# Rotary queries and keys read from PSUM, gains in the tables, and half of a projection moved behind the first attention heads

## What is computed

```
proj = h @ w_in[l]                                   # 1024 -> 1536, split into qa ka va qb kb vb
qa = apply_axial_rope(rms_norm_2(qa, qn_g[l]), cos, sin)    # 8 heads of 64
ka = apply_axial_rope(rms_norm_2(ka, kn_g[l]), cos, sin)    # 2 heads of 64
oa = global_attention(qa, ka, va)                    # softmax of q.k / 8, no mask
ob = window_sink_attention(qb, kb, vb, sink[l], slopes)     # 8 heads, distance bias, a sink
mix = concat(rms(oa), rms(ob)) @ w_o[l]
h = layer_norm(ALPHA * h + mix);  h = layer_norm(ALPHA * h + peer_ffn(h, ...))
```

## Time and profile before

| | |
|---|---|
| median of 3 runs | 2634.62 us |
| the profiled execution: time | 2633.16 us |
| its span | 2631.3 us |
| PE busy | 2512.1 us (95%) |
| DVE busy | 1767.3 us (67%) |
| ACT busy | 1240.7 us (47%) |
| POOL busy | 504.8 us (19%) |
| mean granted TensorE clock | 0.972 |
| HBM | 159 GB/s over the span |

### The profile page before, as it was taken

How to read it: one execution, slowest core, us unless ns; L and a number is a source line. 1 busy time by engine, 2 the same in 40 slices (tenths; PEclk the granted TensorE clock), 3 DMA queues, 4 the chain that set the end, 5 groups by cost and what they waited for, 6 DMA issues and landing times.

```text
span 2631.3 us, 43837 instructions
## 1 busy us (share of the span) xinstructions
PE 2512.1 (95%) x17391; PEld 2262.1 (86%) x17391; DVE 1767.3 (67%) x3113; ACT 1240.7 (47%) x2661; POOL 504.8 (19%) x387
## 2 busy tenths in 40 slices
PE   7898999999899999999999999799999999999997
PEld 6768897998679999999888887679999999888886
DVE  4647334445668975888777556668975888777556
ACT  5441134445345454444555555345454444555554
POOL 3600143544436600000000000536600000000000
PEclk9999799999899999999999999899999999999999
DMA  5400034664324566556678665314566655688664
GB/s 176 134 3 1 25 104 153 185 191 156 109 59 151 163 183 181 184 184 183 208 237 244 198 195 172 112 49 152 163 183 182 184 183 181 207 244 242 197 193 150
DMA packets 146027, 421.09 MB, mean 160 GB/s; under 512 B 15904, under 2 KB 49056, under 8 KB 145440
## 3 DMA queue, kind: packets, MB, share of 16 engines
q1 hardware_dynamic: 142032, 405.34, 50.8%
q0 software_dynamic: 2192, 8.99, 1.0%
q10 hardware_dynamic: 1600, 3.96, 0.4%
HBM read 400.40 MB, written 17.83 MB: 159 GB/s over the span
## 4 chain that ended last, share of the span: by engine, by line
PE 76%; DVE 16%; DMA 3%; ACT 2%; issue 1%; POOL 1%; DVEq 0%; ACTq 0%; SPq 0%
PE pb L418 75%; DMA raw<-in_vT 2%; PE pb L427 2%; DVE arena L2039 1%; DVE arena L2031 1%; DVE arena L2033 1%; DVE arena L2062 1%; DVE arena L2036 1%; DVE arena L2028 1%; DVE arena L1430 1%; DVE arena L1860 1%; ACT hi L1015 1%; DVE arena L1433 1%; DVE lo L1440 1%; DVE arena L1580 1%
## 5 line engine op out<-in xcount | busy, mean ns | idle before, releaser
L1015 ACT CAST hi<-raw 128x512 fp32r<-128x512 f32 x1402 | 815.3, 620 | 409.1 <-DMA raw<-in_vT 187.0
L418 PE MATMUL pb<-HTh,hi 128*128 128x256 f32 (+1 forms) x2968 | 860.6, 290 | 9.9 <-DVE lo L1440 9.9
L418 PE MATMUL pb<-HTl,hi 128*128 128x256 f32 (+1 forms) x2968 | 844.9, 285 | 0.0
L418 PE MATMUL pb<-HTh,lo 128*128 128x256 f32 (+1 forms) x2968 | 844.4, 284 | 0.0
L1440 DVE TENSOR_TENSOR lo<-raw,hi 128x1024 fp32r<-128x1024 f32 x476 | 579.9, 1220 | 92.4 <-ACT hi L1015 92.4
L2201 POOL TENSOR_TENSOR lo<-raw,hi 128x512 fp32r<-128x512 f32 x359 | 487.9, 1382 | 576.7 <-ACT hi L1015 576.2
L418 PEld LDWEIGHTS pb<-HTh,hi 128*128 128x128 f32 x2968 | 573.1, 193 | 12.4 <-issue 10.4
L418 PEld LDWEIGHTS pb<-HTl,hi 128*128 128x128 f32 x2968 | 573.5, 193 | 0.9
L418 PEld LDWEIGHTS pb<-HTh,lo 128*128 128x128 f32 x2968 | 572.5, 193 | 0.0
L418 PE MATMUL pb<-hi,WH 128*128 128x512 f32 x1112 | 434.5, 391 | 7.4 <-DVE WL L2165 7.4
L418 PE MATMUL pb<-lo,WH 128*128 128x512 f32 x1112 | 433.5, 390 | 0.0
(11 more groups left out here) (191 smaller groups left out, 2310.2 us busy)
## 6 DMA issues: line engine op xcount, KB each, us to landing
raw<-in_uT SPq DMA_DIRECT2D x256, 512.0 KB, 3.7
raw<-in_vT SPq DMA_DIRECT2D x256, 512.0 KB, 4.3
raw<-in_w_ffn_in SPq DMA_DIRECT2D x44, 512.0 KB, 3.6
raw<-in_wq SPq DMA_DIRECT2D x32, 512.0 KB, 3.7
wk<-kept SPq DMA_DIRECT2D x128, 128.0 KB, 4.3
raw<-in_w_in SPq DMA_DIRECT2D x24, 512.0 KB, 4.0
raw<-in_w_ffn_out SPq DMA_DIRECT2D x22, 512.0 KB, 4.3
raw<-in_w_gate SPq DMA_DIRECT2D x16, 512.0 KB, 3.5
```

What stands on the lines that cost most here:

```text
L418: return e.matmul(o, l, r, start=start, stop=stop)
L1015: e.copy(u.hi[k], u.half[k]).then_inc(*s.up("hi", ("hi", g)))
```

## The change

- The queries' and keys' rotation reads the projection from PSUM. The gains are multiplied into cosine and sine tables (RC, RS), which POOL makes once a layer (`tables`). The sine part takes two instructions per half instead of four. ACT no longer copies queries and keys; it squares them from PSUM, and for the keys it also sums.
- The queries stay without their norm. Its inverse root goes into the exponential's scale (one value per token and head), and into the factor that makes the negated maximum. In the diff below the programs of PE (`tensor`), ACT (`scalar`), DVE (`vector`) and POOL (`gpsimd`) follow each other; left out are the root, reciprocal and two scalings of the queries, and the keys' mean, rotation, sum and norm, which stand in the same form. The keys are scaled by theirs after the rotation.
- The last two units of the third projection are multiplied in heads 0 and 1; its result goes to banks 4 and 5, and the first attention's output to 6 and 7. The last unit of the second projection comes after the query tiles. The warm matmuls ahead of the heads and in the first two go; tiles 9, 5 to 8 are turned in heads 5 to 9.
- The two broadcast DMAs come after POOL's splits for the projections; one more unit of w_o is cast and split ahead during the heads.
- POOL makes u's low parts up to unit 23; picks run from unit 24 to 48, the gates at 54.

```diff
-            add(("u", l, j), d["uT"][l, j], low=pool if j < 18 else dve)
+            add(("u", l, j), d["uT"][l, j], low=pool if j < 24 else dve)
...
+        self.qneg = self.s2.rearrange("p t h -> p h t")
+        self.RC, self.RS = (T["wk"][:, i * 256:i * 256 + 256].rearrange("p (w t e) -> p w t e", w=2, t=2) for i in range(2))
...
-        project(0, 4)
-        project(1, 6)
...
-        project(2, 0, q_tiles)
+        for g in range(4):
+            project(0, g, 4)
+        for g in range(3):
+            project(1, g, 6)
+        for f in range(4):
+            turn_tile(f, ("qa", l))
+        project(1, 3, 6)
+        for g in range(2):
+            project(2, g, 4)
         turn_tile(4, ("ka", l))
-        warm(5, 6)
...
-            if h < 5:
-                turn_tile((9, 5, 6, 7, 8)[h], ("qb", l))
+            if h < 2:
+                project(2, 2 + h, 4)
+            if 5 <= h < 10:
+                turn_tile((9, 5, 6, 7, 8)[h - 5], ("qb", l))
             if 1 <= h <= 16:
                 at_turn(h - 1)
-                warm((h - 1) % 2, 5)
+                if h > 2:
+                    warm((h - 1) % 2, 5)
...
-            e.copy(m.PJ[:, t, 0:512], PB[4 + t][:, :]).then_inc(*s.up("qkv2", ("pj", l, 0, t)))
+            w.wait_ge(*s.to("q_rope", l, t))
+            fn(m.PJ[:, t, 0:512], PB[4 + t][:, :], ACT.Square).then_inc(*s.up("qkv2", ("pj", l, 0, t)))
...
+            for k in range(2):
+                x = fn(m.PJ[:, t, 512 + 64 * k:576 + 64 * k], PB[6 + t][:, 64 * k:64 * k + 64], ACT.Square, acc=m.ss[:, t, 8 + k:9 + k])
+                x.then_inc(*s.up("qkv2", *([("k_sq", l, t)] if k else [])))
+        w.wait_ge(*s.to("k_ms", l))
+        fn(m.rs[:, :, 8:10], m.s2[:, :, 8:10], ACT.Sqrt).then_inc(*s.up("roots", ("k_root", l)))
+        for t in range(2):
+            w.wait_ge(*s.to("k_rope", l, t))
+            e.copy(m.PJ[:, t, 640:768], PB[6 + t][:, 128:256]).then_inc(*s.up("qkv2", *([("va", l)] if t else [])))
...
-                x = fn(m.PX[i][:, t * 256:(t + 1) * 256], sv[:, t, :], ACT.Exp, bias=m.nmx[:, h, t:t + 1], scale=0.125,
-                       acc=m.den[:, h, t:t + 1])
+                x = fn(m.PX[i][:, t * 256:(t + 1) * 256], sv[:, t, :], ACT.Exp, bias=m.nmx[:, h, t:t + 1],
+                       scale=0.125 if g else m.rs[:, t, h:h + 1], acc=m.den[:, h, t:t + 1])
...
+            if h == 2:
+                second_group()
+            elif h == 9:
+                split_high(units.i + 3)
...
+        def rotate(t, h0, h1, src, which, *done):
+            n = h1 - h0
+            cs = slice(64 * h0, 64 * h1)
+            sx = m.RS[:, which, t, :].rearrange("p (a s i) -> p a s i", a=2, s=2)
+            q5 = src.rearrange("p (h a s i) -> p h a s i", h=n, a=2, s=2)
+            r5 = QR[:, t, cs].rearrange("p (h a s i) -> p h a s i", h=n, a=2, s=2)
+            w.wait_ge(*s.to("tables", l))
+            own()
+            for si in range(2):
+                x = tt(r5[:, :, :, si, :], q5[:, :, :, 1 - si, :], sx[:, :, si, :].unsqueeze(1).to_broadcast([128, n, 2, 16]), M)
+                x.then_inc(*up("rope"))
+            co = m.RC[:, which, t, :].unsqueeze(1).to_broadcast([128, n, 64])
+            tt(heads(QK[:, t, cs], n), heads(src, n), co, M).then_inc(*up("rope", *done))
...
+        for t in range(2):
+            w.wait_ge(*s.to("pj_ps", l, 0, t))
+            rotate(t, 0, 8, PB[4 + t][:, :], 0, ("q_rope", l, t))
+        q_sum()
+        for t in range(2):
+            w.wait_ge(*s.to("pj", l, 0, t))
+            e.tensor_reduce(m.ss[:, t, 0:8], heads(PJ[:, t, 0:512], 8), AXX, A).then_inc(*up("rope"))
+        mean(0, 8, "q_ms")
...
+    tables(0)
     spread(0, m.bc, d["ln_in_g_2"], d["ln_in_b_2"])
     for l in range(2):
-        w.wait_ge(*s.to("turn", ("in", l), 7))
-        spread(2 * l + 1, m.bc1, d["ln1_g_2"][l], d["ln1_b_2"][l])
         for i in range(3):
             for g in range(4):
                 take("win", l, i, g)
+        w.wait_ge(*s.to("turn", ("in", l), 7))
+        spread(2 * l + 1, m.bc1, d["ln1_g_2"][l], d["ln1_b_2"][l])
+        split_low(units.i + 3)
```

More of the change, by code:

```diff
@@ L827, in tensor, with project @@
         turned(("in", l), m.Hv, lambda t, k: ("hn", 2 * l, t, k), range(8), 4, low=False)
[L829 to L846, removed]
+        def project(i, g, b0):
+            u = units.take("win", l, i, g)
+            for k in range(2):
+                c = 2 * g + k
+                for t in range(2):
+                    emptied(b0 + t)
+                    w.wait_ge(*s.to("lo", u.g[k]))
+                    w.wait_ge(*s.to("turn", ("in", l), c))
+                    x = mm3(PB[b0 + t][:, :], m.pair(m.HT, ALL, c, slice(t * 128, (t + 1) * 128)), u.part(k), c == 0, c == 7)
+                    if t == 1:
+                        x.then_inc(*s.up("part", ("part", u.g[k]), *([("pj_ps", l, i, t)] if c == 7 else [])))
+                    elif c == 7:
+                        x.then_inc(*s.up("part", ("pj_ps", l, i, t)))
+                    if c == 7:
+                        free[b0 + t] = [("pj", l, i, t)]
         def turn_tile(f, ready):
@@ L968, in tensor @@
             u_step(j)
-            if j == 50:
+            if j == 54:
                 for p in range(3):
@@ L1298, in scalar, with second_group @@
         take("win", l, 2, 1)
[L1299 to L1308, removed]
+        def second_group():
+            for t in range(2):
+                w.wait_ge(*s.to("pj_ps", l, 2, t))
+                src = PB[4 + t][:, 0:256].rearrange("p (j e) -> p j e", j=4)
+                e.copy(qb[t][:, 1, :, :], src).then_inc(*s.up("qkv2"))
+                e.copy(m.QP[:, t, 1152:1280], PB[4 + t][:, 256:384]).then_inc(*s.up("qkv2", *([("qb", l)] if t else [])))
+                e.copy(m.PJ[:, t, 1408:1536], PB[4 + t][:, 384:512]).then_inc(*s.up("qkv2", ("pj", l, 2, t), *([("vb", l)] if t else [])))
         def at_scores(h):
@@ L1823, in heads @@
             return a.rearrange("p (h e) -> p h e", h=n)
[L1825 to L1831, removed]
         def mean(h0, h1, step):
@@ L2209, in spread, with tables @@
         e.dma_start(bc[:, 1024:2048], b.partition_broadcast(128)).then_inc(*s.up(f"bc{n}", ("bc", n), by=16))
+    def tables(l):
+        co = m.C("cos").rearrange("p (t e) -> p t e", t=2)
+        si = m.C("sin").rearrange("p (t a s i) -> p t a s i", t=2, a=2, s=2)
+        for k in range(2):
+            gain = m.bcs[:, 136 * l + 64 * k:136 * l + 64 * k + 64]
+            ga = gain.rearrange("p (a s i) -> p a s i", a=2, s=2)
+            rs = m.RS[:, k, :, :].rearrange("p t (a s i) -> p t a s i", a=2, s=2)
+            tt(m.RC[:, k, :, :], co, gain.unsqueeze(1).to_broadcast([128, 2, 64]), M).then_inc(*s.up("tables"))
+            for h in range(2):
+                x = tt(rs[:, :, :, h, :], si[:, :, :, h, :], ga[:, :, 1 - h, :].unsqueeze(1).to_broadcast([128, 2, 2, 16]), M)
+                x.then_inc(*s.up("tables", *([("tables", l)] if k and h else [])))
     d = m.d
```

108 lines of the change are left out of this document (45 added, 63 removed).

## The result

The changed kernel takes 2611.05 us (median, 2608.6 to 2613.05), the kernel before in the same runs 2633.36: a ratio of 0.991, 95% interval 0.9888 to 0.9932. It is faster by 22 us, where 59 were forecast (2634.6 - 2576), and lies outside the range. The profiled execution has a span of 2609.9 us, 21.4 less than before.

The account below looks back on a forecast made before the run. PE was taken to bound the kernel, busy 95% of the span. Gains of 21.1 and 21.7 (attention, two layers), 2.6 (output projection) and 13.6 us (experts) sum to 59.0: 2576 us against 2634.6, range 2568 to 2598.

Parts of the forecast that it names:

- POOL's earlier start and the rotation from PSUM: Before the heads: POOL begins 1.3 us earlier, first projection ends T0 (last state split's end) + 7.3; DVE's rotation takes 3.0.
- The query sums: Attention's front, DVE: four sums in POOL's pause take 1.43 us and end 11.9 us after T0.
- rival A: Attention's front: query sums and key products still stall beside POOL's splits, giving 2590 to 2594 us; chance 0.12.
- The queries' scales: Attention's front, DVE: the queries' root, reciprocal and two small scalings end 14.7 us after T0.
- The fourth scores: PE, fourth head: scores end at T0 + 38.3, against 60.1 before in layer 0 and 60.7 in layer 1.
- The softmax scale: Heads, ACT: the exponential's per-partition scale costs 0, covered by ACT's 2.23 us idle before a head's first exponential.
- The expert stage: Experts: six more units split by POOL remove PE's 4.9 us wait and lost clock; 13.6 us gained over two layers.
- Three more tiles ... now lie behind this point, 0.22 each: Heads: five tiles instead of two are turned after the fourth head's scores, costing 0.22 us each.
- The 0.66: Chance given to the forecast of 2576 us, with its own range 2568 to 2585.
- Rival B: Clock: PE's short stops before the heads and missing warm matmuls cost 5 us a layer, giving 2586; chance 0.08.
- no pause of 9 us, so the heads run at 2.4 GHz: Heads: without the former long PE wait the clock stays up; about 6 us of each layer's front gain.
- the output projection, 2.6: Output projection: the third w_o unit, cast and split early, cuts PE's waits for POOL; 2.6 us gained over both layers.

Follow-up runs that it names:

- E4: Changed kernel with the expert stage put back: POOL splits u to unit 17, picks from unit 18, gates at 50; 2622.0 us, ratio 0.9957.
- E1: Changed kernel with only the PSUM bank of the five late tiles changed, to the one the previous head's transposes don't use; 2581.5 us, ratio 0.9804.
- E7: E3 without the third unit of w_o cast or split during the heads; 2579.1 us, ratio 0.9805.
- E5: Changed kernel, shared bank kept, with the warm matmuls put back in the first two heads and ahead of the heads; 2615.7 us, ratio 0.9935.
- E9: Changed kernel, shared bank kept, with nine matmuls on constants placed in the tile waits of heads 6 to 9; 2595.5 us, ratio 0.9861.
- E8: Kernel before the change, with the tiles of heads 1 to 4 moved to the bank the previous head's transposes use; 2653.0 us, ratio 1.0088.
- E2: Changed kernel with only the output projection's banks changed, from 0, 1, 4, 5 to 0, 1, 6, 7; 2606.8 us, ratio 0.9893.
- E12: E1 with only head 6's tile sharing its bank with the transposes of head 5; 2589.4 us, ratio 0.9826.
- E11: E7 with two warm matmuls a head instead of five; 2572.2 us, ratio 0.9767.
- E3: Changed kernel with both bank edits, late tiles (E1) and output projection (E2); 2580.3 us, ratio 0.9792.

## Why the prediction was wrong

**Right.** POOL's earlier start and the rotation from PSUM: T0 + 6.8 and 2.8 us against 7.3 and 3.0. The query sums at 12.6 against 11.9 (rival A's stretch, small: 3.00 instead of 1.43). The queries' scales came at T0 + 17.5 against 14.7; three instructions of 128x16 elements (L1445) beside POOL's splits took 3.1 us of that. The fourth scores at 39.6 and 41.2 against 38.3; of the 2.9 missing in layer 1, 1.7 is a half-clock stretch of 3.4 us at 1648.6. The softmax scale: the exponential grew from 0.47 to 0.56 us and ACT still idles 1.83 before it. The expert stage: 13.9 against 13.6, and E4 gives 14.1 in the traces.

**Wrong: "Three more tiles ... now lie behind this point, 0.22 each".** This is the step that failed. I priced the moved tiles by PE's time alone (0.22 is right: E1's heads with a tile take 3.25, those without 3.03) and did not list what they are queued against: the PSUM bank of each, by head, and the DVE instruction that frees it. The 0.66 was about 15: E1, which changes nothing but the bank, takes back 14.3 and 14.0 a layer, and with it the total, 2581.5, comes within 6 us of the forecast. The loss adds up: 17.1 and 18.6 us a layer are missing up to head 15's scores; 1.3 and 2.9 were missing at the fourth scores, 14.3 and 14.0 are the bank, 1.3 and 1.5 the early unit of w_o (E1 against E7). Rival B had the form (a stretch at half clock in the heads), but put it behind the pauses ahead of the heads and the missing warm matmuls, at 5 us a layer and a chance of 0.08. The pauses ahead of the heads cost 1.7 us of clock at most, the missing warm matmuls were not the cause (E5), and the price was three times as high: 9 us of clock and some 5 of waiting. The sentence "no pause of 9 us, so the heads run at 2.4 GHz" fails with it: two pauses of 0.94 stood before the fall, and PE was busy for 10.11 of the 12 us.

The traces show waits of 0.94 us in successive heads with 24 us at half clock behind them, and none at half clock up to head 15 when the waits are filled or cut to 0.87 (E9). The sentence of the Trainium skill that stands beside rival B ("TensorE: Matmul & The Clock Gate", section "A second HAM failure mode: psum-queue depth-cycling") says of frequent short idle times between groups of matmuls that the clock swings with them; the changed kernel agrees (23.9 us at 0.50 in each layer), E8's layer 1 doesn't (1.00 with four such stops). I weighed it by the rows of before, which had no such waits in the heads; the question was which new ones the moved work would make there.

**Wrong: the output projection, 2.6.** It lost 1.1. Of the 3.7 missing, 2.5 is the same oversight, the swapped output banks meeting OB (1.2 a layer, E2); with it mended 1.4 of the 2.6 is there. Outside this stretch the third unit has a price that I had not counted. I had hidden ACT's casts in its pause, but POOL's split, 2.49 us, stretched DVE's two 128x2 instructions from 0.33 to 1.69 in all, on the chain that paces a head: 1.3 and 1.5 us a layer (E1 against E7), about what the unit brings.

**Not settled.** Why the same waits bring the clock down in one layer and not in the other (E8, E12), and how many it takes. With the four shared banks of the changed kernel it fell in all eight layers of the four traces (changed kernel, E2, E4, E5), but for 17.1 us up to 30.7. Every half-clock stretch over 10 us that began within the heads came behind a stop of PE of 0.9 us or more, but not every such stop made one: E1 has one of 1.2 a layer and E9 two of 0.87, without a fall in the heads. That was seen, not controlled. Half-clock stretches of 10.2 us behind the heads, in one layer each of E1, E4, E9 and E11, have no explanation here.

## What to carry to other kernels

When work moves along a software pipeline, write down for each moved item which buffer it uses at its new place, who used it last there, and which instruction frees it; an alternation by index (f%2 against h%2) changes sides with an odd shift. Price a short wait of TensorE in a stretch of small matmuls at its length and at what a lower clock may cost behind it: here some 5 and 9 us a layer. Where such a wait couldn't be removed, matmuls on constants placed inside it held the clock (nine, E9); the five that the changed kernel has elsewhere in each of these heads did not.

## What the runs showed that I had not expected

- The clock fell to half behind 12 us in which PE was busy for 10.11, with two stops of 0.94; in E8, layer 1, it stayed up with PE busy for 22.22 of 26 us and four such stops.
- POOL's split also stretches the smallest DVE instructions, and not only those with two inputs in SBUF: one of 128x2 elements with a single tile as input went from 0.17 to 1.20 us (E7, E3). The prediction had said it of two inputs alone.
- Of warm matmuls a head, five are more than needed here and none too few, with both banks mended and the early unit gone: 2579 us with five, 2572 with two, 2573 to 2598 with none. What they do in the traces is fill a stop: head 9 stops for 1.11 us with none, 0.3 with two, and not at all with five.
